# Mixed layer of a transformer kernel: rotations on VectorE, compression copies on ScalarE, packed up-projections

## What is computed

```python
q = (rmsnorm(c_q, q_norm) @ w_uq).reshape(b, s, 6, 64 + 32)        # MLA: six heads, 64 plain + 32 rotated
q_pe = rope(q[..., 64:], pos, 32)
kv = (rmsnorm(c_kv, kv_norm) @ w_ukv).reshape(b, s, 6, 64 + 64)    # k_nope and v, six heads
k_pe = rope(k_rope[:, :, None, :], pos, 32)                        # one rotated key for all heads
...
q = rope(q, pos, 16); k_cmp = rope(k_cmp, pos, 16)                 # NSA: 16 of 64 dimensions rotate
k_sel = rope(k_sel, pos, 16); k_win = rope(k_win, pos, 16)
chunks = x.reshape(b, s // 16, 16, g, d)                           # compress_blocks, for k_cmp and v_cmp
blocks = jnp.concatenate([chunks[:, :-1], chunks[:, 1:]], axis=2) + pos_emb
return jax.nn.gelu(flat @ w1) @ w2
...
# rope: [x1 * cos - x2 * sin, x2 * cos + x1 * sin] on the two halves of the rotated part
```

## Time and profile before

| | us |
|---|---|
| median of 3 runs | 2912.34 (2910.73 to 2913.3) |
| profiled execution | 2909.54 |
| its span | 2907.6 |
| TensorE busy | 2806.2 (97%) |
| VectorE busy | 1771.2 (61%) |
| ScalarE busy | 1119.3 (38%) |
| mean granted clock of TensorE | 0.988 |

### The profile page before, as it was taken

One profiled execution on the slowest core, in us unless ns is written; L12 is line 12 of the kernel. 1 busy time (PEld: TensorE's weight loads), 2 busy tenths in 40 slices (PEclk: granted clock), 3 DMA queues, 4 the chain that ended last, 5 costly groups with the idle time before them and its releaser, 6 DMA issues.

```text
span 2907.6 us, 35115 instructions
## 1 busy us (share of the span) xinstructions
PE 2806.2 (97%) x13162; PEld 2239.7 (77%) x13162; DVE 1771.2 (61%) x2676; ACT 1119.3 (38%) x1646; POOL 60.3 (2%) x38
## 2 busy tenths in 40 slices
PE   8999999999999999999999999999999999979996
PEld 6888877577788887888877577688887888767784
DVE  5566553675555666556653575555557754478896
ACT  4122232477412214122132377422224444357775
POOL 0000000000000000000000000000000000011220
PEclk9999999999999999999999999999999999989998
DMA  7223333200332223322243100232223313279995
GB/s 198 87 87 115 94 72 72 51 6 26 116 101 87 87 81 122 101 87 87 82 98 81 39 1 26 87 114 95 95 72 99 86 59 86 72 275 365 366 364 227
DMA packets 236681, 324.56 MB, mean 112 GB/s; under 512 B 59072, under 2 KB 204616, under 8 KB 224160
## 3 DMA queue, kind: packets, MB, share of 16 engines
q1 hardware_dynamic: 229232, 309.94, 32.7%
q0 software_dynamic: 5584, 11.02, 1.4%
q10 hardware_dynamic: 1760, 2.23, 0.2%
HBM read 317.39 MB, written 14.16 MB: 114 GB/s over the span
## 4 chain that ended last, share of the span: by engine, by line
PE 86%; DVE 5%; DMA 3%; issue 2%; ACT 2%; SPq 1%; DVEq 1%; ACTq 0%; POOLq 0%
PE score L952 11%; PE score L954 11%; PE score L953 11%; PE acc L1302 8%; PE acc L1005 7%; PE acc L983 5%; PE acc L985 5%; PE acc L984 5%; PE acc L1058 3%; PE score L1039 3%; PE acc L1490 3%; PE score L1490 2%; PE turn L1047 2%; PE acc L997 1%; DMA arena<-in_expert_w_gate 1%
## 5 line engine op out<-in xcount | busy, mean ns | idle before, releaser
L2148 DVE SCALAR_TENSOR_TENSOR x_T<-acc,x_T 128x512 f32<-128x512 f32 x352 | 243.1, 691 | 404.4 <-PE acc L985 404.0
L952 PE MATMUL score<-h_hi,gate_hi 128*128 128x512 f32 x704 | 275.1, 391 | 8.6 <-DVE gate_lo L2053 8.5
L952 PE MATMUL score<-h_hi,up_hi 128*128 128x512 f32 x704 | 275.6, 391 | 0.0
L953 PE MATMUL score<-h_lo,gate_hi 128*128 128x512 f32 x704 | 274.4, 390 | 0.0
L954 PE MATMUL score<-h_hi,gate_lo 128*128 128x512 f32 x704 | 274.4, 390 | 0.0
L954 PE MATMUL score<-h_hi,up_lo 128*128 128x512 f32 x704 | 273.9, 389 | 0.0
L953 PE MATMUL score<-h_lo,up_hi 128*128 128x512 f32 x704 | 273.9, 389 | 0.0
L983 PE MATMUL acc<-hid_hi,down_hi 128*128 128x512 f32 x640 | 250.4, 391 | 2.0 <-DVE x_T L2148 1.6
L984 PE MATMUL acc<-hid_lo,down_hi 128*128 128x512 f32 x640 | 249.1, 389 | 0.0
L985 PE MATMUL acc<-hid_hi,down_lo 128*128 128x512 f32 x640 | 249.1, 389 | 0.0
L1669 ACT ACTIVATE exp_tile<-probs 128x512 f32<-128x512 f32 x88 | 50.8, 625 | 409.3 <-DVE probs L2119 409.3
(11 more groups left out here) (455 smaller groups left out, 6044.2 us busy)
## 6 DMA issues: line engine op xcount, KB each, us to landing
weights<-in_ffn_w_gate SPq DMA_DIRECT2D x44, 1024.0 KB, 5.3
weights<-in_ffn_w_up SPq DMA_DIRECT2D x44, 1024.0 KB, 5.3
weights<-in_ffn_w_down SPq DMA_DIRECT2D x44, 1024.0 KB, 5.5
arena<-in_expert_w_gate SPq DMA_DIRECT2D x32, 1024.0 KB, 7.4
arena<-in_expert_w_up SPq DMA_DIRECT2D x32, 1024.0 KB, 7.0
weights<-in_expert_w_down SPq DMA_DIRECT2D x30, 1024.0 KB, 6.6
weights<-in_w_in SPq DMA_DIRECT2D x23, 1024.0 KB, 5.3
weights<-in_w_out SPq DMA_DIRECT2D x6, 1024.0 KB, 5.0
```

The lines of the kernel that those rows point to most:

```text
L952: mm(ps, hi[:, kc, cols], h_hi[:, kc, :], start=kc == 0, stop=False, skip_group_check=True)
L953: mm(ps, hi[:, kc, cols], h_lo[:, kc, :], start=False, stop=False, skip_group_check=True)
L2148: V.scalar_tensor_tensor(x_T[:, c, :], acc[c % 2][:, :], 0.25, x_T[:, c, :], ALU.mult, ALU.add).then_inc(acc_free[c % 2], 1)
```

## The change

It makes 34 entries out of 54. (1) The 13 rope entries go. VectorE makes the swapped halves with stream_shuffle, whose pattern of 32 partitions is the same in every quarter, and the sine table takes the sign. For nq, kc, ks, kw and kr this is the function turn_pairs, placed after later entries by ROPE_AFTER. The rotated parts of the queries are now a projection of their own. (2) xs_v and xs_k go. ScalarE copies halves of nk into `pairs` behind the entries ks (for v) and kw (for k), sorted so that compress reads runs of contiguous columns; a counter xs_ready tells of it. (3) uq becomes un (three, 128 rows = the plain parts of two heads) and ur (128 and 64 rows = the rotated parts of four and two heads); kn is packed to three. For that w_uq comes by four transfers and w_ukv by two. ScalarE evacuates un and kn in two halves; VectorE rotates ur and writes q6 with one addition per head. The rotated key is copied to the six heads of k6 behind sv 1. (4) The position embeddings come by four transfers, cmp is two entries, compress for k runs in one piece.

```diff
-    + [("sq", 0, 7, "dve"), ("rope", 10, None, "dve"), ("sq", 1, 7, "dve"), ("xs_v", 0, None, "act")]
...
-    + [("rope", 6, None, "dve"), ("mv", 2, 13, "act"), ("mv", 3, 13, "act"), ("cmp", 0, None, "act")]
+    + [("sq", 0, 7, "dve"), ("sq", 1, 7, "dve"), ("sk", 0, 8, "dve"), ("sk", 1, 8, "dve")]
+    + [("sv", 0, 9, "act"), ("sv", 1, 9, "act"), ("ur", 0, 12, "dve"), ("un", 0, 12, "act"), ("ur", 1, 12, "dve")]
+    + [("un", 1, 12, "act"), ("un", 2, 12, "act"), ("kn", 0, 13, "act"), ("kn", 1, 13, "act"), ("kn", 2, 13, "act")]
+    + [("mv", 0, 13, "act"), ("mv", 1, 13, "act"), ("mv", 2, 13, "act"), ("mv", 3, 13, "act")]
+    + [("cmp", 0, None, "act"), ("cmp", 1, None, "act")]
...
-COMPRESS_AFTER = {("sk", 1): (1, 0, 8), ("rope", 8): (1, 8, 16), ("sv", 1): (0, 0, 8), ("rope", 11): (0, 8, 16)}
-GELU_IN_AT = {("rope", 9): 1, ("rope", 0): 0}
-GELU_AT = {("sv", 1): 1, ("uq", 2): 0}
-GELU_OUT_AT = {("rope", 12): 1, ("rope", 2): 0}
+COMPRESS_AFTER = {("sk", 1): (1, 0, 8), ("sv", 0): (1, 8, 16), ("sv", 1): (0, 0, 16)}
+GELU_IN_AT = {("sv", 1): 1, ("un", 0): 0}
+GELU_AT = {("sv", 1): 1, ("un", 1): 0}
+GELU_OUT_AT = {("ur", 0): 1, ("un", 2): 0}
+LAST_TICKET[10] = TICKET["sv", 1]
+LAST_TICKET[11] = TICKET["ur", 0]
+ROPE_AFTER = {("vc", 0): "kc", ("ks", 0): "nq0", ("vsw", 0): "nq1", ("vsw", 1): "nq2", ("sq", 0): "kr", ("sq", 1): "ks",
+              ("sk", 0): "kw"}
+SWAP_MLA = [i ^ 16 for i in range(32)]
+SWAP_NSA = [i ^ 8 for i in range(16)] + list(range(16, 32))
...
                     elif n == 12:
-                        sp.dma_start(s3(s, 2, 576), w_uq[l]).then_inc(w_loaded[s], 16)
+                        for kc in range(2):
+                            for at_, d0, d1 in ((0, 0, HD), (384, HD, 96)):
+                                sp.dma_start(s3(s, 2, 576)[:, kc, at_:at_ + 6 * (d1 - d0)].rearrange("p (h x) -> p h x", h=6),
+                                             w_uq[l][:, kc, :].rearrange("p (h x) -> p h x", h=6)[:, :, d0:d1]
+                                             ).then_inc(w_loaded[s], 16)
...
                         m = mm(turn[kv][:, 0:93].rearrange("p (g w) -> p g w", g=3), w1[:, c, :],
-                               src.rearrange("p (g t) -> p g t", t=S)[:, :, 0:481:16], start=c == 0, stop=c == 15)
+                               pairs[kv][:, :, c % 8, c // 8:c // 8 + 31], start=c == 0, stop=c == 15)
...
+                    elif name in ("ur", "un"):
+                        w = s3(s, 2, 576)[:, :, slice(P * i, P * i + P) if name == "un" else slice(
+                            384 + P * i, min(512 + P * i, 576))]
+                        for kc in range(2):
+                            m = mm(ps[0:w.shape[2], :], w[:, kc, :], lora[:, kc, :], start=kc == 0, stop=kc == 1)
...
+                        elif name in ("un", "kn"):
+                            for g in range(2):
+                                t = (q6 if name == "un" else k6)[0:HD, 2 * i + g, :]
+                                m = fn(t, acc[n % 2][g * HD:(g + 1) * HD, :], ACT.Copy,
+                                       scale=Q_SCALE if name == "un" else 1.0)
...
+                    if name in ("ks", "kw"):
+                        kv = name == "ks"
+                        if kv:
+                            taken(act, l, BM, TICKET["vc", 0])
+                        else:
+                            act.wait_ge(rope_ready, at(l, N_ROPE, 1))
+                        for g in range(2):
+                            src = nk[g * HD:(g + 1) * HD, 3 if kv else 0, :].rearrange("p (i r s) -> p s r i", r=8, s=2)
+                            for q in range(2):
+                                m = fn(pairs[kv][q * HD:(q + 1) * HD, g, :, :], src[:, q, :, :], ACT.Copy)
+                        m.then_inc(xs_ready, 1)
...
+                def turn_pairs(which):
+
+                    dve.drain()
+                    if which == "kr":
+                        r, t = slice(HD, 96), lora[HD:96, 3, :]
+                        V.stream_shuffle(rt[r, :], t, SWAP_MLA)
+                        cos, sin = cst("cos_mla")[r, :], cst("sin_mla")[r, :]
+                    else:
+                        r, t = slice(0, P), ROPES[which]
+                        V.stream_shuffle(rt[:, :], t, SWAP_NSA)
+                        cos, sin = cst("cos_nsa"), cst("sin_nsa")
+                    dve.drain()
+                    V.tensor_tensor(t, t, cos, ALU.mult)
+                    V.tensor_tensor(rt[r, :], rt[r, :], sin, ALU.mult)
+                    dve.drain()
+                    if which in ("ks", "kw"):
+                        own, other = K_TILE["sel" if which == "ks" else "win"]
+                        dve.wait_ge(xs_ready, at(l, 2, 2))
+                        V.tensor_tensor(nk[HD:P, other, :], t[HD:P, :], rt[HD:P, :], ALU.add)
+                        V.tensor_tensor(nk[0:HD, own, :], t[0:HD, :], rt[0:HD, :], ALU.add)
+                        V.memset(nk[0:HD, other, :], 0.0)
+                        dve.drain()
+                        V.memset(nk[HD:P, own, :], 0.0).then_inc(rope_ready, 1)
+                    elif which == "kr":
+                        V.tensor_tensor(t, t, rt[r, :], ALU.add)
+                    else:
+                        V.tensor_tensor(t, t, rt[:, :], ALU.add).then_inc(rope_ready, 1)
...
+                    elif name == "ur":
+                        rows, tmp = (P, HD)[i], et[:, 0, :]
+                        V.stream_shuffle(rt[0:rows, :], ps[0:rows, :], SWAP_MLA)
+                        V.scalar_tensor_tensor(tmp[0:rows, :], ps[0:rows, :], Q_SCALE, cst("cos_mla", rows=rows),
+                                               ALU.mult, ALU.mult).then_inc(acc_free[n % 2], 1)
                         dve.drain()
+                        V.scalar_tensor_tensor(rt[0:rows, :], rt[0:rows, :], Q_SCALE, cst("sin_mla", rows=rows),
+                                               ALU.mult, ALU.mult)
+                        dve.drain()
+                        for g in range(rows // 32):
+                            r = slice(32 * g, 32 * g + 32)
+                            m = V.tensor_tensor(q6[HD:96, 4 * i + g, :], tmp[r, :], rt[r, :], ALU.add)
+                        m.then_inc(rope_ready, 1)
+                        dve.drain()
...
+                    if (name, i) in ROPE_AFTER:
+                        turn_pairs(ROPE_AFTER[name, i])
+                    if (name, i) == ("sv", 1):
+                        dve.wait_ge(acc_full, mix_full(l, n + 1))
+                        V.tensor_copy(k6[HD:96, :, :], lora[HD:96, 3, :].unsqueeze(1).broadcast_to([32, 6, S])
+                                      ).then_inc(rope_ready, 1)
...
-            V.memset(arena[:, cmp_in[1] + 2 * S:18000], 0.0)
+            V.memset(arena[:, 16384:18000], 0.0)
```

More of the change, by code:

```diff
@@ L71, in constant_table, with rope @@
     pos = np.arange(S, dtype=np.float32)
-    def rope(rows, start, half):
+    def rope(start, half):
         freq = np.float32(500000.0) ** (-np.arange(half, dtype=np.float32) / np.float32(half))
         ang = (pos[:, None] * freq[None, :].astype(np.float32)).astype(np.float32).T
-        rot = np.zeros((rows, rows), np.float32)
-        c, s = np.ones((rows, S), np.float32), np.zeros((rows, S), np.float32)
+        c, s = np.ones((P, S), np.float32), np.zeros((P, S), np.float32)
         for b in start:
-            for i in range(half):
-                rot[b + half + i, b + i] = -1.0
-                rot[b + i, b + half + i] = 1.0
             c[b:b + 2 * half] = np.concatenate([np.cos(ang), np.cos(ang)])
[L83 to L88, removed]
+            s[b:b + 2 * half] = np.concatenate([-np.sin(ang), np.sin(ang)])
+        return c, s
+    for name, args in (("mla", ((0, 32, 64, 96), 16)), ("nsa", ((0, 64), 8))):
+        c, s = rope(*args)
         put("cos_" + name, c)
@@ L298, in build @@
         sv = view(TB, 256)
-        pairs, pos_at, cmp_in = [], [], []
+        pairs, pos_at = [], []
+        off[0] = 16384
         for _ in range(2):
[L302 to L306, removed]
+            pairs.append(view(3, 256).rearrange("p g (r i) -> p g r i", i=32))
+            pos_at.append(pairs[-1][:, 2, :, 0:2].rearrange("p r h -> p h r"))
+        assert off[0] <= 18000
         off[0] = 2048
@@ L730, in mix_loads @@
                     elif n == 12:
-                        sp.dma_start(s3(s, 2, 576), w_uq[l]).then_inc(w_loaded[s], 16)
+                        for kc in range(2):
[3 more added lines that the diff above has]
+                                             ).then_inc(w_loaded[s], 16)
                     elif n == 13:
-                        sp.dma_start(s3(s, 1, 768), w_ukv[l]).then_inc(w_loaded[s], 16)
+                        for t in range(2):
+                            sp.dma_start(slot[s][:, 384 * t:384 * t + 384].rearrange("p (h x) -> p h x", h=6),
+                                         w_ukv[l][:, 0, :].rearrange("p (h t x) -> p h t x", h=6, t=2)[:, :, t, :]
```

(16 more changed lines are left out.)

85 lines of the change are left out of this document (18 added, 67 removed).

## The result

The changed kernel takes 2866.34 us (median of 4 runs, 2862.09 to 2870.5) against 2911.53 for the kernel before on the same chip (4 runs, 2905.37 to 2913.3). The ratio is 0.984, 95% interval 0.9824 to 0.9857. The forecast was 2871.5, range 2862 to 2882. The profiled execution took 2865.21 us, 44.3 less than the profiled one of before.

The account below looks back on a forecast made before the run. The prediction took TensorE's matmuls in the two mixed layers as the bound. Removed matmuls and waits less new stalls, walked entry by entry, gave 20.4 us per layer, 40.8 in all: 2912.3 − 40.8 = 2871.5 us, range 2862 to 2882.

Parts of the forecast that it names:

- sq 0 to first up-projection: Dense part before ur 0: 56.4 us less six rotations, four selections and two evacuation waits, 44.2 us left.
- up-projections to attention: From ur 0 at 512.2 through un, kn, mv and cmp to attention at 533.2, with a 3.2 us stall at un 2.
- won ahead of attention: Layer 0's first attention score moves from 553.83 to 533.2: 20.6 us, less 0.2 for the shuffle's pattern, 20.4 per layer.
- clock: Half-clock stretches even: one less in attention's opening, one more behind one of the two pauses; chance 0.50.
- Removed matmuls: TensorE, per layer: rotations 12.3 us, selections 4.3, uq 1.8 and kn 3.0 saved, 21.4 in all.
- The two new pauses: TensorE waits about 3.0 us at sq 0 for kw's evacuation and 3.2 at un 2 for ur 1's bank.
- The shuffle: On VectorE, priced like another 128x512 operation: 0.69 us, 0.76 from start to start, plus 0.2 per layer for its pattern.
- Rival B: VectorE is the bound because shuffles cost twice (1.4 us): 18.3 us saved per layer, 2875.7; chance 0.16.
- rival C: Kernel slower: six shuffles in the evacuation queue, about 5 us slack together, 6 us each gives 2925; chance 0.04.
- Costed at nothing: the compression: Compression matmuls now read contiguous columns: at most 2.6 us per layer might be won, 0 taken.
- Costed at nothing: the rest: ScalarE's strided copies (0.4 us each), the k6 copy (3.35 at most) and weight transfers all stay hidden.
- rival A's mild end: Neither new pause brings half clock and attention's opening gains 2.5 us: 22.9 per layer, 2866.5; chance 0.11.

Follow-up runs that it names:

- layout experiment: Against the changed kernel, pairs is laid out by token again, so compress reads with a stride of eight elements: 2871.78 us, ratio 0.987.
- late-copy experiment: Against the changed kernel, the copy to k6 comes behind mv 3, made twice, and the first cmp waits for it: 2876.17 us, ratio 0.989.
- one control: The changed kernel run again unaltered, beside the kernel with nq 2's rotation behind kw: 2863.95 us, ratio 0.9835.
- the other control: The changed kernel run again unaltered, beside the kernel with nq 2's rotation behind the gates: 2867.36 us, ratio 0.9851.

## Why the prediction was right

The forecast of 2871.5 lies 5.2 over the median of 2866.34: 40.8 us were forecast, 45.2 came. The mechanism is the forecast one. In the layers themselves the distance is larger than in the medians: the traces have 48.5 for both layers where 40.8 were forecast, and the rest of the program took some 4 us more in that execution. So part of the closeness is luck. Step by step, for layer 0:

| step | forecast, us | measured, us |
|---|---|---|
| start of sq 0, later by (from cq) | 2.5 | 81.09 − 78.47 = 2.6 |
| sq 0 to first up-projection | 44.2 | 511.23 − 469.33 = 41.9 |
| up-projections to attention | 533.2 − 512.2 = 21.0 | 532.54 − 511.23 = 21.3 |
| won ahead of attention | 20.6, then 20.4 | 22.4 |
| clock | even | +2.2 in the opening, −1.7 behind sq 0 (inside the 41.9) |

**Removed matmuls.** Right. The path was TensorE's, six matmuls put back cost 0.88 each, and the up-projections kept their price (16 records in 7.40, 0.46 each, against 1.96 for four). The selections, the packing and the rotations of the tail were not put back by themselves; that their terms hold rests on the sums in the table.

**The two new pauses.** Right in place, cause and size: 3.10 (about 3.0 forecast) and 3.05 (3.2). The walk of VectorE's queue holds to a few tenths: bank of kw free at 469.2, where 467.95 was forecast for a layer that began 1.1 earlier.

**The shuffle.** 0.72 to 0.76 with a pattern of 0.01, forecast 0.69 and 0.2 for the pattern. Rival B's condition (1.4) did not hold. The experiment with three shuffles shows what it would have cost: 5.6 us of waits per layer for 1.66 more on each. The 5 us of slack of rival C lie in kr, ks and kw alone; nq 2, ur 0 and ur 1 have none.

**Costed at nothing: the compression.** This is the term that was mis-sized. The text itself had bounded it (0.12 against 0.16 a record, at most 2.6 us) and took 0. The records came to 0.11, and 3.2 us per layer were won, beyond that bound too, 6.4 in all: most of the 7.7 by which the traces of the layers lie past the forecast. The stride explains it, as the layout experiment shows. In the dense part 0.8 stay unassigned (44.2 − 3.2 + 1.7 = 42.7 against 41.9).

**Costed at nothing: the rest.** The copy to k6 took 1.75 and not 3.35 (a copy, not an addition with two inputs), hidden all the same behind 4.35 us of idle time. ScalarE's copies took 0.63 to 0.67, against 0.4 taken and 0.9 allowed, hidden. The slack at sv 0 was 2.6 us (bank free at 491.92, sv 0 at 494.52) and not 3.6: the half clock put off both the bank and sv 0, but the compression ahead of sv 0 was faster by 0.8. w_uq's four transfers landed in 3.3 to 3.4 us.

**The clock.** Even was forecast. In the first profile it is +0.5 a layer: 2.2 back in the opening, 1.7 lost behind the first pause, nothing behind the second. So the profile lies between the forecast and rival A's mild end. That the figure of that end, 2866.5, is within 0.2 of the median is luck: its condition, no half clock behind either pause, did not hold. The late-copy experiment shows that the 2.2 hang on the wait at cmp. The likeliest case came about, with the compression's gain on top.

## What to carry to other kernels

Where two PSUM banks alternate, as here, work that is put off on the evacuating engine belongs behind the evacuations of both banks that TensorE wants next, not only of the one that shows the wait: behind kw it won 1.0 us a layer, one entry later 2.0. Walk the queue of the evacuating engine entry by entry; it gave both pauses within 0.2 us, and where the walk was not made (kn 0 on VectorE) the pause only changed place. And when a layout changes, look at the step between the elements that TensorE reads, above all where the matmuls are narrow and the sorting can be done by an engine with idle time.

## What the runs showed of the hardware

- **fp32 matmuls of 93 columns** took 0.11 us a record with runs of 31 adjacent columns, 0.17 with a stride of 32 bytes and 0.16 with one of 64 bytes. The stride alone makes it half as much again (the layout experiment).
- **The clock behind a pause of 3 us.** All 16 passages through the first pause (3.1 us, in one kernel 4.8; eight profiled executions with two layers each) were followed by a stretch at 0.50: 3.4 us in 12 of them, 6.8 in 4. Behind the second (2.9 to 3.1 us at un 2) it fell in 7 of 16 passages, among them both of one control, and none of the other control or of the first profile. The length of the pause alone does not decide it; what does is open. The Trainium skill ("TensorE: Matmul & The Clock Gate", Part 1) has the clock low after idling, and the first pause and the wait at cmp agree; the second shows that it is no certain price.
- **A copy and an addition of the same shape** on VectorE, 32x3072: 1.75 us and 3.35. The Trainium skill ("VectorE: DVE Perf Modes", the perf-mode tier table) has a `tensor_copy` of fp32 in SBUF at double rate and a `tensor_tensor` at single rate; the two rows agree.
